# Seven block products for eight in the feed-forward down projections of the second block

## The reference, cut to what matters

```
def swiglu(u, w1, w3, w2):                 # u (256, 1024), w1, w3 (1024, 2816), w2 (2816, 1024)
    return (silu(u @ w1) * (u @ w3)) @ w2

for l in range(2):
    h = h + 0.5 * swiglu(rms_norm_2(h, ffn1_norm[l]), ffn1_w1[l], ffn1_w3[l], ffn1_w2[l])
    h = h + token_mixer(...)
    h = h + 0.5 * swiglu(rms_norm_2(h, ffn2_norm[l]), ffn2_w1[l], ffn2_w3[l], ffn2_w2[l])
return rms_norm_2(h, final_norm)
```

## Time and profile before

| | |
|---|---|
| median of 3 runs | 1527.72 us (1527.14 to 1528.8) |
| the profiled execution | 1526.78 us, span 1525.0 us |
| mean granted TensorE clock | 0.997 |
| TensorE busy | 1494.8 us, 98% of the span |
| VectorE busy | 828.7 us, 54% |
| ScalarE busy | 716.2 us, 47% |
| GpSimd busy | 98.3 us, 6% |

### The profile page before, as it was taken

How to read it: one execution, slowest core, us unless ns; L and a number is a source line. 1 busy time by engine, 2 the same in 40 slices (tenths; PEclk the granted TensorE clock), 3 DMA queues, 4 the chain that set the end, 5 groups by cost and what they waited for, 6 DMA issues and landing times.

```text
span 1525.0 us, 20880 instructions
## 1 busy us (share of the span) xinstructions
PE 1494.8 (98%) x7748; PEld 1142.2 (75%) x7748; DVE 828.7 (54%) x1120; ACT 716.2 (47%) x1193; POOL 98.3 (6%) x166
## 2 busy tenths in 40 slices
PE   8999999999999999999999999999999999999998
PEld 7886335887433888888888888888888888888886
DVE  5675225576324655555766554565455566755544
ACT  5673223674213544445655444454444537454443
POOL 2321001231000000002000000000000100000000
PEclk9999999999999999999999999999999999999999
DMA  7739995547899555556345666656555643565551
GB/s 251 261 130 393 371 419 213 205 166 300 354 422 332 193 186 181 190 194 199 105 166 190 197 192 192 188 169 194 187 188 182 217 144 116 201 207 182 191 192 56
DMA packets 166054, 328.36 MB, mean 215 GB/s; under 512 B 8906, under 2 KB 106960, under 8 KB 153056
## 3 DMA queue, kind: packets, MB, share of 16 engines
q1 hardware_dynamic: 164992, 323.52, 60.7%
q0 software_dynamic: 992, 3.89, 0.9%
HBM read 326.33 MB, written 1.05 MB: 215 GB/s over the span
## 4 chain that ended last, share of the span: by engine, by line
PE 92%; DVE 3%; ACT 3%; DVEq 1%; issue 1%; DMA 1%; POOL 0%; SPq 0%; POOLq 0%; ACTq 0%
PE bank L475 24%; PE bank L477 23%; PE bank L476 23%; PE bank L1278 7%; PE bank L1327 4%; PE bank L903 1%; PE bank L1336 1%; PE bank L978 1%; DMA sb_raw<-w_in 1%; PE bank L1447 1%; PE bank L1069 1%; ACT sb_whi L464 1%; PE bank L1487 1%; PE bank L1515 0%; PE bank L1507 0%
## 5 line engine op out<-in xcount | busy, mean ns | idle before, releaser
L471 DVE TENSOR_TENSOR sb_wlo<-sb_raw,sb_whi 128x1024 fp32r<-128x1024 f32 (+1 forms) x417 | 479.9, 1194 | 321.8 <-ACT sb_whi L464 321.4
L464 ACT ACTIVATE sb_whi<-sb_raw 128x1024 fp32r<-128x1024 f32 (+2 forms) x419 | 408.1, 1028 | 295.5 <-PE bank L477 286.0
L475 PE MATMUL bank<-sb_whi,sb_op_hi 128*128 128x512 f32 (+2 forms) x1212 | 474.1, 391 | 3.4 <-DVE sb_op_lo L2089 1.7
L477 PE MATMUL bank<-sb_whi,sb_op_lo 128*128 128x512 f32 (+2 forms) x1212 | 466.3, 385 | 0.0
L476 PE MATMUL bank<-sb_wlo,sb_op_hi 128*128 128x512 f32 (+2 forms) x1212 | 465.5, 384 | 0.0
L475 PEld LDWEIGHTS bank<-sb_whi,sb_op_hi 128*128 128x128 f32 x1212 | 228.1, 188 | 49.9 <-issue 2.1
L477 PEld LDWEIGHTS bank<-sb_whi,sb_op_lo 128*128 128x128 f32 x1212 | 227.8, 188 | 45.9
L476 PEld LDWEIGHTS bank<-sb_wlo,sb_op_hi 128*128 128x128 f32 x1212 | 228.3, 188 | 42.4
L475 PE MATMUL bank<-sb_whi,sb_lat_hi 128*128 128x512 f32 (+2 forms) x456 | 175.7, 385 | 1.0 <-DVE sb_wlo L471 1.0
L477 PE MATMUL bank<-sb_whi,sb_lat_lo 128*128 128x512 f32 (+2 forms) x456 | 174.5, 383 | 0.0
L476 PE MATMUL bank<-sb_wlo,sb_lat_hi 128*128 128x512 f32 (+2 forms) x456 | 174.4, 382 | 0.0
(11 more groups left out here) (283 smaller groups left out, 1335.2 us busy)
## 6 DMA issues: line engine op xcount, KB each, us to landing
sb_raw<-ffn_w SPq DMA_DIRECT2D x264, 512.0 KB, 4.3
sb_raw<-w_in SPq DMA_DIRECT2D x84, 512.0 KB, 4.6
sb_moe<-exp_w_gate_up SPq DMA_DIRECT2D x36, 1024.0 KB, 11.9
sb_moe<-exp_w_down SPq DMA_DIRECT2D x18, 1024.0 KB, 11.5
sb_raw<-w_out SPq DMA_DIRECT2D x32, 512.0 KB, 4.3
sb_own<-exp_w_gate_up SPq DMA_DIRECT2D x12, 1024.0 KB, 8.5
sb_per_block<-exp_w_gate_up SPq DMA_DIRECT2D x4, 1024.0 KB, 4.9
sb_xg<-exp_w_gate_up SPq DMA_DIRECT2D x4, 1024.0 KB, 9.6
```

Of the source, the lines that this page charges most:

```text
L464: nc.scalar.activation(h, r, ACT.Copy).then_inc(hi_made.sem, 1)
L471: on.tensor_tensor(o, r, h.bitcast(F32), ALU.subtract).then_inc(lo_made.sem, 1)
L475: nc.tensor.matmul(ps, hi, wh, start=first, stop=False)
L477: return nc.tensor.matmul(ps, lo, wh, start=False, stop=last)
```

## The change

In 10 of the 11 units of every run (`NS`) the down projection is done as a 2 x 2 by 2 x 2 block product with seven block products (Winograd's form of Strassen's scheme) in place of eight: A is the transposed activations (blocks of 128 hidden columns x 128 tokens), B the w2 slab (blocks of 128 x 512). Each product now has an accumulator of its own over the run, seven banks (0 to 3, 5, 6, 7), so that bank 4 alone is left for both up chunks and for the transposes in turn. The eleventh unit keeps its eight products (`last_down`).

- The operands need sums: four of B (`weight_sums`, 128x512 each, VectorE, from `raw` to `t_raw`), four of A (`sums_of_a`, 128x128 each, VectorE). Their high parts are made by ScalarE (`t_part`, two of 128x1024; one of 128x896 for the seven A operands), their low parts by VectorE (`operands_lo`). Of the slab itself three of four blocks are split (`direct_hi`, `direct_lo`: 128x512 and 128x1024).
- TensorE's up projection goes by chunk (`up_by_chunk`): all 24 matmuls of chunk 0, then of the down projection before it products 1, 2, 3, then 24 matmuls of chunk 1, products 4 and 5, the transposes, products 6 and 7.
- The raw w2 slab's load waits for `down_read`, which comes when `direct_lo` is done (`down_early`), and stands ahead of the next unit's up loads in SyncE's order.
- At the end of a run VectorE joins the products: a copy and two sums from banks 3, 5, 6, and six additions to `x` (`halved`).

Core of the diff:

```diff
+FAST = {1: (A11, (0, 0), None, 3), 2: (A12, (1, 0), None, 0), 3: (S4_OF_A, (1, 1), None, 1), 4: (A22, None, T4_OF_B, 2),
+        5: (S1_OF_A, None, T1_OF_B, 7), 6: (S2_OF_A, None, T2_OF_B, 5), 7: (S3_OF_A, None, T3_OF_B, 6)}
...
@@ SyncE
+                def down_early(number, j, u):
+                    slot, run = j % RING, j0 // S2_FFN2
+                    wait_down = G["down_read"]
+                    sp.wait_ge(wait_down.sem, wait_down.after(l, u + run * NS))
...
-                with sp.Fori(1, NU2) as u:
+                up(slab_number(BASE2, S2, l, j0 + 2), j0 + 2, 1)
+                down(slab_number(BASE2, S2, l, j0 + 4), j0 + 4, 0)
+                with sp.Fori(2, NU2) as u:
                     j = u * 3 + (j0 - 1)
+                    down_early(slab_number(BASE2, S2, l, j + 2), j0 + 4, u - 1)
                     up(slab_number(BASE2, S2, l, j), j0 + 2, u)
-                    down(slab_number(BASE2, S2, l, j + 2), j0 + 4, u - 1)
...
@@ TensorE
+            def fast_down(slot, names, opening=False, closing=False):
+
+                for name in names:
+                    of_a, direct, of_b, b = FAST[name]
+                    w = tile(slot, D, 1, direct[0], 512 * direct[1], 512) if direct else (t_hi[:, of_b, :], t_lo[:, of_b, :])
+                    i = products(bank[b][:, :], mix_a_hi[:, of_a - 1, :], mix_a_lo[:, of_a - 1, :], *w, opening, closing)
+                return i
...
+                up_by_chunk(S, l, num(j0 + 2), up_slot, 1, n0, lambda ch: bank[HB + ch], second_ready,
+                            lambda: unit_transposes(S, l, n0 + 1, first_up_bank(n0, 1), mixed))
+                a_ready(1)
+                fast_down(down_slot, (1, 2, 3), True).then_inc(S["direct_done"].sem, 1)
+                slab_ready(num(j0 + 4))
+                fast_down(down_slot, (5,), True)
+                unit_transposes(S, l, n0 + 2, bank[HB], mixed)
+                fast_down(down_slot, (4, 6, 7), True).then_inc(slab_done.sem, 1)
...
                 with pe.Fori(2, count - 1) as u:
+                    def first_part():
+                        a_ready(u)
+                        fast_down(down_slot, (1, 2, 3)).then_inc(S["direct_done"].sem, 1)
+
                     j = u * 3 + (j0 - 1)
-                    unit_up(num(j), (j0 + 2) % RING, S["h_c0"], None, paired)
-                    unit_down(S, l, num(j + 2), (j0 + 4) % RING, u + n0, by_chunk)
-                    unit_transposes(S, l, 0, u + (n0 + 1))
+                    up_by_chunk(S, l, num(j), up_slot, u, n0, lambda ch: bank[HB], up_ready(u), first_part)
+                    slab_ready(num(j + 2))
+                    fast_down(down_slot, (4, 5))
+                    unit_transposes(S, l, u + (n0 + 1), bank[HB], mixed)
+                    fast_down(down_slot, (6, 7)).then_inc(slab_done.sem, 1)
...
+                up_by_chunk(S, l, num(j), up_slot, u, n0, lambda ch: bank[HB], up_ready(u), last_parts)
+                fast_down(down_slot, (5,), closing=True)
+                fast_down(down_slot, (2,))
+                unit_transposes(S, l, n0 + count, bank[HB], plain)
+                fast_down(down_slot, (3, 4)).then_inc(slab_done.sem, 1)
...
@@ ScalarE
+                silu(1, num(j0 + 3), (0,))
+                turned_in(0, first_up_bank(n0, 1))
+                operands_hi(0)
+                ahead(j0 + 2, 1, (0,))
+                silu(1, num(j0 + 3), (1,))
+                ahead(j0 + 2, 1, (1,))
+                ahead(j0 + 3, 1)
+                turned_in(1, bank[HB])
+                wait(S, "direct_done", l, run * NS + 1)
+                direct_hi(1)
+
+                with act.Fori(2, count - 1) as u:
+                    operands_hi(u - 1)
+                    silu(u, num(u * 3 + j0), (0,), one)
+                    wait(S, "direct_done", l, u + run * NS)
+                    direct_hi(u)
                     ahead(j0 + 2, u)
+                    silu(u, num(u * 3 + j0), (1,), one)
+                    ahead(j0 + 3, u, (0,))
+                    turned_in(u, bank[HB])
+                    ahead(j0 + 3, u, (1,))
...
@@ VectorE
+                    tt(t1, b12, b11, ALU.subtract)
+                    tt(t3, b22, b12, ALU.subtract)
+                    dve.drain()
+                    tt(t2, b22, t1, ALU.subtract)
+                    dve.drain()
+                    tt(t4, b21, t2, ALU.subtract).then_inc(S["t_made"].sem, 1)
...
                 activations(0, (1,), lambda ch: first_up_bank(n0, ch))
                 ahead(j0 + 3, 0, (1,))
+                weight_sums(0)
+                direct_lo(0)
+                wait(S, "aT", l, n0 + 1)
+                activations(1, (0,))
+                sums_of_a(0)
+                operands_lo(0)
+                activations(1, (1,))
+                ahead(j0 + 2, 1)
+                ahead(j0 + 3, 1, (0,))
+                sums_of_a(1)
+                ahead(j0 + 3, 1, (1,))
+                weight_sums(1)
+                direct_lo(1)
+
+                with dve.Fori(2, count - 1) as u:
+                    operands_lo(u - 1)
+                    activations(u, (0,), one)
+                    weight_sums(u)
+                    direct_lo(u)
                     ahead(j0 + 2, u)
+                    activations(u, (1,), one)
+                    ahead(j0 + 3, u, (0,))
+                    sums_of_a(u)
+                    ahead(j0 + 3, u, (1,))
...
+                operands_lo(u - 1)
+                activations(u, (0,), one)
+                slab_is_done(number(u - 1) - 2)
+                p1, u2, u3 = (joint[:, i, :] for i in range(3))
+                nc.vector.tensor_copy(p1, bank[3][:, :])
+                dve.drain()
+                tt(u2, bank[5][:, :], p1, ALU.add)
+                halved(0, 0, p1)
+                dve.drain()
+                tt(u3, bank[6][:, :], u2, ALU.add)
+                halved(0, 1, u2)
+                dve.drain()
+                halved(1, 0, u3)
+                halved(1, 1, u3)
+                ahead(j0 + 2, u)
+                activations(u, (1,), one)
...
+                slab_is_done(number(u - 1))
+                halved(0, 1, bank[7][:, :])
+                halved(1, 1, bank[7][:, :])
+                dve.drain()
```

More of the change, by code:

```diff
@@ L896, in unit_up, with unit_transposes, up_by_chunk, last_down @@
                 slab(number + 1, (slot + 1) % RING, 512, range(4, 8), to, False, True, h_signal, before=before, paired=paired)
[L898 to L908, removed]
+            def unit_transposes(S, l, n, to, order):
+                wait(S, "a", l, 2 * n)
+                for i, (ch, f) in enumerate(order):
+                    t = nc.tensor.transpose(to[:, i * P:i * P + P], av[:, ch, f * P:f * P + P], ident)
+                t.then_inc(S["aT"].sem, 1)
+            def up_by_chunk(S, l, number, slot, u, n0, banks, ready, between):
+                for ch in range(NC):
+                    ready(ch)
+                    for s in range(2):
+                        at = (slot + s) % RING
+                        if ch == 0:
+                            slab_ready(number + s)
+                        for k in range(4):
+                            t, tok = 4 * s + k, slice(ch * P, ch * P + P)
+                            i = products(banks(ch)[:, :], op_hi[:, t, tok], op_lo[:, t, tok], *tile_pair(at, k), t == 0, t == DK - 1)
+                        if ch == 1:
+                            i.then_inc(slab_done.sem, 1)
+                    if ch == 0:
+                        i.then_inc(S["h_c0"].sem, 1)
+                        between()
+            def last_down(S, l, number, slot, n, parts, between):
+                wait(S, "a_lo", l, n)
                 slab_ready(number)
@@ new lines, in direct_lo, with t_part @@
+                def direct_lo(u):
+                    wait(S, "direct_hi", l, u + (run * NS + 1))
+                    for part in (slice(0, 512), slice(D, 2 * D)):
+                        i = tt(wlo[slot][:, part], raw[slot][:, part], whi[slot][:, part].bitcast(F32), ALU.subtract)
+                    i.then_inc(S["down_read"].sem, 1)
+                def t_part(u, part):
+                    two = slice(2 * part, 2 * part + 2)
+                    dve.wait_ge(hi_made.sem, number(u) * 2 + (part + 1))
+                    tt(t_lo[:, two, :], t_raw[:, two, :], t_hi[:, two, :].bitcast(F32), ALU.subtract).then_inc(lo_made.sem, 1)
@@ L2066, in units_lo, with operands_lo @@
+                def operands_lo(u):
+                    t_part(u, 0)
+                    wait(S, "a_hi", l, u + (n0 + 1))
+                    tt(mix_a_lo[:, :, :], a_parts[:, A11:S4_OF_A + 1, :], mix_a_hi[:, :, :].bitcast(F32), ALU.subtract).then_inc(S["a_lo"].sem, 1)
+                    t_part(u, 1)
+                one = lambda ch: bank[HB]
                 activations(0, (0,))
```

149 lines of the change are left out of this document (100 added, 49 removed).

## The result

The changed kernel takes **1573.31 us** (median of 4 runs, 1571.42 to 1576.01), the kernel before beside it 1527.59: ratio 1.0301, 95% interval 1.0288 to 1.0313. Slower, as forecast, but by 45.7 us and not by 21.3 (1549, range to 1565). The profiled span went from 1525.0 to 1574.2; the profiled execution is the slowest of the four (1576.01).

The account below looks back on a forecast made before the run. TensorE's matmul stream was taken as the bound (busy 98%). Waits of 45 us and 4 of clock, less 27.2, made +21.8 on the profiled 1526.78, 1548.6; with 0.94 for the median, 1549 us, range 1524 to 1565.

Parts of the forecast that it names:

- matmuls removed: TensorE's stream: 3 matmuls fewer in each of 10 units of 4 runs, 120 x 0.227 = 27.2 us saved.
- first transposes (loads): Head of a run: unit 1's transposes wait 1.0 us for a product delayed by late up-slab loads.
- bank 4: Head of a run: the copy freeing this bank stands behind the sixth load's high part, a wait of 1.3 us.
- A low part: Head of a run: the second trip's first products wait 3.75 us for this operand, behind VectorE's queued work.
- last transposes: Tail of a run: VectorE's joining stands ahead of chunk 1's product, so the transposes wait 3.6 us.
- behind the last transposes: Tail of a run: the last unit's low part waits 0.2 us, the first residual parts are held by 0.5.
- the loop: Steady trips: 16.1 us each with no wait, VectorE fitting at 14.4 but with no slack at the transposes.
- next trip's transposes, and clock: Behind the head: second trip's transposes wait 0.9 us a run; slower clock behind long gaps costs 4 in all (0 to 8).
- rival 2: Loop: VectorE bounds it, each instruction starting only as the former ends; +13 us, or 1562; chance 0.14.
- Rival 3: TensorE's stream: the products have a slower pitch, 0.25 in place of 0.227; +19 us, or 1568; chance 0.04.
- Rival 1: Head of a run: it isn't late, costing 2.5 us, with the tail 3.5; 1524.5, faster; chance 0.2.
- The rule in the prediction: VectorE: the next instruction doesn't start until the pipe of the one before is empty; the loop would be short of time.

Follow-up runs that it names:

- e2: The changed kernel with the joining at a run's tail waiting only for the last unit's own three products, no longer for the slab's release: 1558.49 us.
- e10: e8 with the operands mixed from A put in the latent tensors' place in SBUF: 1531.74 us.
- e11: e10 with chunk 1's product taken between the two low parts of the slab in the last unit too: 1525.41 us, ratio 0.9983 to the kernel before.
- e1: The changed kernel with SyncE issuing unit 2's up slabs ahead of unit 1's w2 slab at a run's head: 1551.85 us.
- e8: e6 with VectorE, in the loop, taking chunk 1's product between the two low parts of the first up slab, not behind both: 1532.04 us.
- p3: The changed kernel with the operands mixed from A put in the latent tensors' place in SBUF: 1569.88 us (one run).
- e5: The changed kernel with 10, 14 and 14 zero-adding 128-column matmuls ahead of the three long waits of each run, to keep TensorE busy: 1569.73 us.
- e7: e6 with unit 1's weight sums on GpSimd, its A low part ahead of its T low parts, and two joining additions behind the last low part: 1550.11 us.
- p2: The changed kernel with the operands mixed from A moved to the start of their SBUF region, in 8 tiles each: 1572.77 us (one run).
- p4: The changed kernel with the mixed operands in their own place but holding the up operand's values: 1570.9 us (one run).
- e6: The changed kernel with the edits of e1 and e2 together: 1537.35 us.
- e9: e8 with two of the joining's additions moved behind the last unit's low part: 1535.94 us.

## Why the prediction was half right

The direction and the places were right; the size was off by 24 us, outside the range. In the profiled execution, for four runs in us (27 off, as it is the slowest of its kernel):

| term | forecast | measured |
|---|---|---|
| matmuls removed | -27.2 | -27.2 |
| first transposes (loads) | 4.0 | 11.0 |
| bank 4 | 5.2 | 5.4 |
| A low part | 15.0 | 14.4 |
| last transposes | 14.4 | 14.4 |
| behind the last transposes | 2.8 | 3.6 |
| the loop | 0 | 11 |
| next trip's transposes, and clock | 3.6 + 4 | 0.3 + 13.8 |
| sum | +21.8 | +47, of 49.2 |

The 3.6 is read from e2, whose tails have no slow matmul, the 13.8 is what 69 slow matmuls took beyond 0.23 each. Some 2 us are left unassigned. Two slips of the sum are small: it makes 1549.5 and not 1549, and 63 matmuls are 14.30 and not 14.28. Term by term:

- **Removed: right.** Trips of 16.14 in e10 and 16.12 in e11, with 16.1 forecast, show that a matmul less is 0.227 less.
- **The A low part, 3.75 a run: right.** 3.6 in each. So are bank 4 (1.3; 1.37, 1.45, 1.26, 1.36) and the last transposes (3.6; 3.59). The 0.2 and 0.5 behind these come as 0.18 and 0.86 at the second run's tail, where no matmul was slow:

```profile
1023.65 0.40 PE L489 MATMUL bank<-sb_t_hi,sb_mix_a_lo 128*128 128x512 f32 x1
1024.06 0.50 PE L487 MATMUL bank<-sb_whi,sb_lat_hi 128*128 128x512 f32 x1
...
1028.05 0.39 PE L489 MATMUL bank<-sb_whi,sb_lat_lo 128*128 128x512 f32 x1
1028.76 0.44 PE L1533 MATMUL bank<-sb_const,sb_x 128*128 128x128 f32 x2 [0.32 <-DVE sb_x L2673]
1029.36 0.88 PE L1533 MATMUL bank<-sb_const,sb_x 128*128 128x128 f32 x6 [0.16 <-DVE sb_x L2673]
```

- **Loads ahead of the first transposes, 1.0 a run: the step that failed first.** 3.5, 2.0, 2.7 and 2.8, 11.0 in all, +7. I had the third load landing 6.2 behind direct_lo's end (840.2 to 846.4), with all six going out together. They don't: SyncE issued them 0.5 to 1.0 apart. In the second run the third went out 1.4 behind direct_lo's end and took 5.8 more (854.3 to 861.41, 7.1), and in the others 7.8 to 8.6 in all. The mechanism, SyncE stuck behind direct_lo, was right: e1 takes it away and 21.5 us with it. That is more than the waits it ends (11.0 + 5.4); the A low part's wait shrinks too (0.6 a run), and 38 matmuls are slow, not 71.
- **"No wait in the loop, and no slack at the transposes": the step that failed second.** I put the product's end at 14.3 of the trip and the due time at 14.28. It ended at 14.46 (903.62 in a trip from 889.16), and a due time is earlier than I took it: the transposes' operand load runs 0.22 ahead of them. The late load costs 0.12 a trip; e8 gives back 0.10. This is rival 2's place, but not its cause: VectorE's pairs of low parts still take 2.36, against 2.35 in the earlier trace rows.
- **Matmul pitch, "the same for two kinds of operands": the third.** The matmuls of block products were 0.234 apart, which with the up matmuls between them is 0.14 a trip. Rival 3 had 0.25 and a chance of 0.04. Its cause was the operand's place, which no row of before could have shown, since there the place was the quick one (p3). The two loop terms together are +11 (0.3 a trip, 0.39 in the third run, where the transposes come 0.09 later still; e8 ends that too).
- **Next trip's transposes, 0.9, and clock, 4 in all: the fourth, +7 together.** I took half of the clock's loss; the gaps made it fall in 7 of 8 places, and once more at the first transposes. The two are one loss, seen in two ways. At the tails a slow matmul is lost time: 27 of them are 5.4 us, and e5 and e2 both give 5.4 and 5.3 back. At the heads it hides VectorE's own lateness: the changed kernel waits at the second trip's transposes in one run only (0.3), while in e5, with the clock up, that wait is 1.3 to 2.6 in every run, where I had 0.9. So the clock alone is worth the 3.6 to 6.9 that e5 gives, near the forecast; what I had too small is VectorE's lateness behind the A low part.

Rival 1 (head not late) fell: e1 still has 3.0 of it. A rule of the Trainium skill bears on e7. The Trainium skill, "SBUF — State Buffer", section "Who interferes with whom", says that a VectorE instruction with two SBUF inputs contends with a GpSimd instruction that reads SBUF, and that this contention is an exclusive lock. The 6.49 beside GpSimd's sums, against 3.49 alone, agrees. The rule in the prediction, from the Trainium skill, "VectorE: DVE Perf Modes", section "The DRAIN you can't avoid", is borne out no better than there: no pair of independent low parts takes longer than before (2.36). The section itself adds what the prediction left out, that a next instruction which is not held starts earlier.

## What to carry over

A wait in a loop's head or tail is worth as much as several us of arithmetic saved in its body: write out both by the queue, and for every DMA order what stands behind the wait that is put ahead of it. Slack at a consumer counts from the load of its operand, not from its start. And slow-clock matmuls behind a wait are to be priced by what comes next: where nothing waits for the engine that was late, as at the tails here, each is lost time; where the same engine is due again soon, as at the heads, they mostly hide its lateness, and only keeping the clock up shows what they cost.

## What the runs showed of the hardware

- Matmuls of 512 columns with their stationary operand in one region of SBUF start 0.234 apart, in another 0.227, with the same contents and the same writers (p3 against the changed kernel); moving within the first region changed nothing (p2), nor did other contents (p4). The up products between such blocks are slower too (24 in 5.47 to 5.48, against 5.44 in p3).
- VectorE and GpSimd, both on SBUF operands: 6.49 for what takes 3.49.
- A plain fp32 matmul of 128 columns is two records of 0.12 each (28 records in 3.29 us).
- The length of a gap alone didn't settle whether the granted clock fell. Of 16 gaps of 3.20 to 3.22 (the heads of e1, e6, e8, e9) it stayed up behind seven, of 8 of 3.34 to 3.35 (e10, e11) behind one. In the changed kernel it stayed up behind 3.73 and 3.81, and fell behind 2.95; in e2 it fell behind 2.60:

```profile
860.14 0.66 PE L925 MATMUL bank<-sb_const,sb_unit_work 128*128 128x128 f32 x4 [2.21 <-DVE sb_unit_work L2184]
...
861.30 0.63 PE L489 MATMUL bank<-sb_t_hi,sb_mix_a_lo 128*128 128x512 f32 x1
861.72 0.63 PE L487 MATMUL bank<-sb_t_hi,sb_mix_a_hi 128*128 128x512 f32 x1
```
